# Two rows of the modulation's first quarter weighted by TensorE products instead of VectorE

## What is computed

```python
mod = jax.nn.silu(c) @ ada_w[layer] + ada_b[layer]          # (1, 1024) @ (1024, 6144)
shift1, scale1, gate1, shift2, scale2, gate2 = jnp.split(mod[:, None, :], 6, axis=-1)
h = rmsnorm(x, norm1_w[layer]) * (1 + scale1) + shift1
... = jnp.split(h @ w_in[layer], split_at, axis=-1)
```

## Time and profile before

| | |
|---|---|
| median of 3 runs | 894.42 us (894.19 to 894.9) |
| the profiled execution | 894.87 us |
| its span (first to last instruction) | 893.1 us |
| TensorE busy | 876.5 us, 98% |
| VectorE busy | 498.3 us, 56% |
| ScalarE busy | 365.6 us, 41% |
| DMA, mean over the span | 127 GB/s |

### The profile page before, as it was taken

One profiled execution on the slowest core, in us unless ns is written; L12 is line 12 of the kernel. 1 busy time (PEld: TensorE's weight loads), 2 busy tenths in 40 slices (PEclk: granted clock), 3 DMA queues, 4 the chain that ended last, 5 costly groups with the idle time before them and its releaser, 6 DMA issues.

```text
span 893.1 us, 13455 instructions
## 1 busy us (share of the span) xinstructions
PE 876.5 (98%) x5425; PEld 749.0 (84%) x5425; DVE 498.3 (56%) x599; ACT 365.6 (41%) x464; POOL 37.6 (4%) x40
## 2 busy tenths in 40 slices
PE   6999999999999999999999999999999999999997
PEld 5998878899898988888888898888888888888886
DVE  6778884646473748423445666555555556433337
ACT  6551226784534372522223344333333333322234
POOL 0010000000000000000122300000000000000004
PEclk9999999999999999999999999999999999999999
DMA  9975745115352454342424423333333332422202
GB/s 323 316 251 164 201 97 164 49 48 189 114 170 94 144 188 154 132 150 85 142 95 141 131 60 95 94 94 94 94 94 94 94 94 94 134 101 94 94 0 96
DMA packets 117141, 113.03 MB, mean 127 GB/s; under 512 B 7412, under 2 KB 107126, under 8 KB 114663
## 3 DMA queue, kind: packets, MB, share of 16 engines
q1 hardware_dynamic: 116375, 110.21, 39.6%
q10 hardware_dynamic: 720, 2.16, 0.7%
HBM read 104.80 MB, written 4.21 MB: 122 GB/s over the span
## 4 chain that ended last, share of the span: by engine, by line
PE 88%; DVE 4%; DMA 3%; SPq 2%; ACT 1%; issue 1%; DVEq 0%; ACTq 0%
PE bank L1835 25%; PE bank L1836 25%; PE bank L1837 25%; PE bank L2342 1%; PE bank L2176 1%; DMA ada_in<-in_ada_w_dram 1%; SPq L520 1%; PE bank L2016 1%; PE bank L2104 1%; PE bank L2181 1%; PE bank L2144 1%; DMA raw<-in_w_in_dram 1%; PE bank L1989 1%; PE bank L1870 1%; PE bank L2011 1%
## 5 line engine op out<-in xcount | busy, mean ns | idle before, releaser
L1835 PE MATMUL bank<-h_hi,w_hi 128*128 128x512 f32 x672 | 264.2, 393 | 0.9 <-DVE w_lo L1274 0.9
L1837 PE MATMUL bank<-h_hi,w_lo 128*128 128x512 f32 x672 | 261.6, 389 | 0.0
L1836 PE MATMUL bank<-h_lo,w_hi 128*128 128x512 f32 x672 | 261.6, 389 | 0.0
L1835 PEld LDWEIGHTS bank<-h_hi,w_hi 128*128 128x128 f32 x672 | 126.2, 188 | 27.5 <-DVE w_lo L1274 1.1
L1837 PEld LDWEIGHTS bank<-h_hi,w_lo 128*128 128x128 f32 x672 | 126.1, 188 | 26.5
L1836 PEld LDWEIGHTS bank<-h_lo,w_hi 128*128 128x128 f32 x672 | 126.2, 188 | 25.6 <-issue 0.2
L1267 DVE TENSOR_TENSOR w_lo<-raw,w_hi 128x2048 fp32r<-128x2048 f32 (+2 forms) x44 | 81.0, 1852 | 88.6 <-ACT w_hi L694 88.6
L1274 DVE TENSOR_TENSOR w_lo<-raw,w_hi 128x2048 fp32r<-128x2048 f32 x31 | 71.1, 2293 | 86.4 <-ACT w_hi L702 86.4
L1774 DVE SCALAR_TENSOR_TENSOR conv<-bank,vecs,conv 128x511 f32<-128x511 f32 x88 | 65.6, 748 | 66.2 <-ACT conv L1108 60.7
L702 ACT ACTIVATE w_hi<-raw 128x2048 fp32r<-128x2048 f32 x31 | 59.1, 1907 | 69.3 <-PE bank L1837 69.3
L694 ACT ACTIVATE w_hi<-raw 128x2048 fp32r<-128x2048 f32 (+2 forms) x42 | 67.9, 1631 | 44.4 <-DMA raw<-in_w_in_dram 34.7
(11 more groups left out here) (272 smaller groups left out, 1227.5 us busy)
## 6 DMA issues: line engine op xcount, KB each, us to landing
raw<-in_w_up_dram SPq DMA_DIRECT2D x44, 512.0 KB, 4.7
raw<-in_w_in_dram SPq DMA_DIRECT2D x17, 1024.0 KB, 5.3
raw<-in_ada_w_dram SPq DMA_DIRECT2D x16, 1024.0 KB, 5.5
raw<-in_w_in_dram SPq DMA_DIRECT2D x22, 512.0 KB, 5.6
raw<-in_w_down_dram SPq DMA_DIRECT2D x22, 512.0 KB, 4.2
ada_in<-in_ada_w_dram SPq DMA_DIRECT2D x16, 512.0 KB, 9.5
raw<-in_w_gla_branch_dram SPq DMA_DIRECT2D x4, 1024.0 KB, 5.1
raw<-in_w_out_dram SPq DMA_DIRECT2D x4, 1024.0 KB, 5.2
```

Source lines behind the costliest of these rows:

```text
L1835: pe.matmul(out_ap, wh, xh, start=first, stop=False, skip_group_check=True)
L1836: pe.matmul(out_ap, wh, xl, start=False, stop=False, skip_group_check=True)
L1837: return pe.matmul(out_ap, wl, xh, start=False, stop=last, skip_group_check=True)
```

## The change

For quarter 0, blocks 6 and 7 are taken off VectorE and put into `DIRECT[0]`. `FIRST_SUMS` now ends with block 5 in both halves, so VectorE does 6 instead of 8 steps per half. In `first_shift_scale` TensorE first takes, once silu(c) and the second half of the quarter are there, blocks 6 and 7 with their columns of `c_silu` (2 blocks x 2 column groups x 4 strips = 16 matmuls per half), then waits for VectorE's step of block 5, and sums block 0 with the ones as before. No transfer and no instruction of ScalarE, GpSimd or SP is changed.

```diff
-DIRECT = {1: range(5, KT), 2: range(6, KT), 3: range(0)}
-ADA_STEPS = [2 * KT] + [KT - len(DIRECT[j]) for j in range(1, KT // 2)]
-FIRST_SUMS = [(0, range(0, 4)), (1, range(0, 2)), (0, range(4, 8)), (1, range(2, 3)), (1, range(3, 8))]
+DIRECT = {0: range(6, KT), 1: range(5, KT), 2: range(6, KT), 3: range(0)}
+ADA_STEPS = [2 * (KT - len(DIRECT[0]))] + [KT - len(DIRECT[j]) for j in range(1, KT // 2)]
+FIRST_SUMS = [(0, range(0, 4)), (1, range(0, 2)), (0, range(4, 6)), (1, range(2, 3)), (1, range(3, 6))]
...
             def first_shift_scale(kk):
 
                 pe.wait_ge(ones_set, 1)
-                pe.wait_ge(ada_step, FIRST_AT[kk, KT - 1])
+                pe.wait_ge(silu_done, 1)
+                pe.wait_ge(ada_landed[1], 32)
                 if kk > 0:
                     pe.wait_ge(first_mod, 1)
-                for n in (kk, kk + 2):
-                    last = column_sum(bank[7], n, ada_rows(0, 0)[:, n * P:(n + 1) * P], ones[:, 0:1], n == 0, True)
+                for row in (*DIRECT[0], 0):
+                    if row == 0:
+                        pe.wait_ge(ada_step, FIRST_AT[kk, DIRECT[0][0] - 1])
+                    for n in (kk, kk + 2):
+                        last = column_sum(bank[7], n, ada_rows(0, row)[:, n * P:(n + 1) * P],
+                                          ones[:, 0:1] if row == 0 else c_silu[:, row:row + 1],
+                                          n == 0 and row == DIRECT[0][0], row == 0)
                 last.then_inc(first_ps if kk == 0 else mod1_ps, 1)
```

## The result

| | before | changed |
|---|---|---|
| median, same chip | 894.79 us (20 runs, 893.79 to 895.42) | 894.89 us (20 runs, 894.04 to 901.0) |
| profiled execution, span | 894.87, 893.1 | 894.97, 893.2 |

The ratio is 1.0026 (95% interval 1.0016 to 1.0037): the change makes the kernel slower by 0.26%, though its median hardly moves. The reason is in the single executions, and no number of this kernel can be understood without it: eleven of the 20 took 894.04 to 894.97 us (median 894.29, that is 0.5 less than before), nine took 899.5 to 901.0 (median 900.43), and nothing lay between. The mean of all 20 is 897.06 against 894.72 before, which is the 0.26%. Their mean granted clock differs too, 0.998 to 1.000 against 0.994 to 0.996. No execution of the kernel before, in five groups of 20 to 31, was above 895.8.

A forecast was written before the change was run, and what follows sets the result against it. The prediction took TensorE, busy 98% of the span, as the bound; -1.01 + 0.27 - 0.27 + 0.73 = -0.3 us took the median from 894.42 to 894.1 us, with an 8-in-10 range of 893.2 to 895.0.

The forecast's parts named there:

- Step 1, half 0: Quarter 0's first column sum: two VectorE rows fewer let TensorE start 1.01 us earlier; 32 added records cost 0.27 us.
- the 25 ns of the Trainium skill: Minimum start-to-start distance of matmuls; by it the 32 added records would cost 0.8 us per half, an estimate of 894.7.
- Step 2, half 1: Quarter 0's second column sum: no gain, 0.27 us added to TensorE, swallowed by 0.47 us of slack in the wide product.
- Step 3, who stops the shift: Start of quarter 1: weight landings fixed at 25.91 and 28.89 us cut the 1 us gain to 0.28 us.
- my wait: Quarter 1: new waits for landings, VectorE 0.6 to 0.9 us before L1191, TensorE about 0.5 us before L1870.
- my first rival: Quarter 1's landings don't hold; landing 0.8 us earlier, the whole 1.0 us comes through: 893.4 us; chance 0.13.
- Step 4: From quarter 1's sums to the end: everything behind moves by the same 0.3 us, and no DMA is added.
- anything else, the clock among it: Rival for any other cause, such as a fall from the granted 2.4 GHz; no size given; chance 0.02.
- The sum: Whole kernel: -1.01 (half 0) + 0.27 - 0.27 (half 1) + 0.73 (waits for fixed landings) = -0.3 us.

The follow-up runs named there:

- half 1 alone: The change made only in half 1, blocks 6 and 7 of half 0 staying on VectorE, against the kernel before; 895.86 us, ratio 1.0017.
- the products alone: The kernel before plus the 16 added products per half, sent to columns nobody reads, with all eight VectorE steps kept; 894.2 us, ratio 0.9995.
- before padded: The kernel before with 128 waits for a semaphore long set (64 instructions) at the start of TensorE's program; 895.9 us, ratio 1.0017.
- half 0: As a run: the change made only in half 0, half 1 as in the kernel before; 895.56 us, ratio 1.0012.
- the merged version without SP's wait: The change only in the first half, idle transposes at four places merged into wider products, SP's transfers not held back; 894.2 us, ratio 0.9995.
- the late kernel: The changed kernel with two of five idle transposes ahead of half 1's column sums replaced by one 512-column product; 894.24 us, ratio 0.9997.

## Why the prediction was wrong

The forecast was no difference; I gave 0.93 to "within 0.2%" and 0.04 to slower, and it is slower by 0.26%. The median, 894.89, lies in the range, but that is little comfort, since it stands between two groups that it describes badly.

**Step 1, half 0: the price was right, the occasion was not.** 32 added records cost 0.28 us (I had 0.27 from quarter 1's 8.4 ns), and the 25 ns of the Trainium skill that I weighed against it is not seen here. The wait of 1.11 us that they were to fill is a matter of the execution. It was 1.11 where TensorE started at 6.7 us, 0.39 in the second trace of before, where it started at 7.6, and in the traces of the changed kernel the start was 6.9 to 8.1. In the profiled execution of the changed kernel the tokens' transposes, not VectorE, come last at this place, and the 1.0 us of the step was worth nothing (16.70 for the transposes, 18.05 for the sum). With an early start (6.9, the execution of 893.16 us) the order came as forecast: the added products began at 16.93, the ones at 17.20. But VectorE's rows began earlier there too, at 15.32. In both traces of before the column sum came 2.20 us after that start (15.74 to 17.94, 15.95 to 18.15), so all eight steps would have let TensorE go at 17.52 there (an estimate), and the gain is 0.3 us, not 1.0. No trace of the changed kernel shows the full one. I took one trace's slack for the kernel's.

**Step 2, half 1: right.** From the start of half 1's sums to that of quarter 1's sums TensorE takes 29.39 - 22.14 = 7.25 us before, 29.51 - 22.25 = 7.26 with the change and 29.31 - 22.05 = 7.26 with half 1 alone, the added 0.27 us included. The slack behind it swallows them. The total of half 1 alone doesn't test the step: its trace has a stall of 1.65 us at an edge near 44 us, which is more than its 1.1 us of loss.

**Step 3, who stops the shift: not seen in any trace, and the landings aren't fixed.** In none of the five traces of the changed kernel does VectorE's first row of quarter 1 or TensorE's first product there wait for a landing. In the profiled execution VectorE began quarter 1 at 26.24 and the sums at 29.51, at about the old places, which was the late start and not my wait. In the execution of 893.16 us the landings, by issue plus time to landing, were 25.06 and 28.14 against my 25.91 and 28.89. VectorE began at 25.39 and the sums at 28.66, without a wait. The stream of weights isn't fixed from one execution to the next; the two landings moved by 0.85 and 0.75 us. This was my first rival (0.13), and its 893.4 is near that one execution, though the 1.0 us that it lets through wasn't there.

**Step 4 is the step that failed.** It said that nothing is added to DMA, and that everything behind moves by the same 0.3 us. TensorE's 128 more instructions are themselves brought by DMA, half a block of 256, and they moved the edges of the blocks against the work. The count was in sight ("32 records" for 16 calls, and the instruction queue is a line of the page), but I counted instructions only by the time that they run. The edge moved from 39.9 us, where its block had begun to come 8 us ahead, to 30.8 us, where the block comes 0 to 0.3 us late in short executions and 3.7 us late in the long one that was traced. Padding shows that the place of an edge alone can cost time: 64 instructions that do nothing made the kernel before slower by 0.17%, with a stall of 1.54 us at an edge predicted ahead. And with the edge moved out of the sums by the same padding the changed kernel had no long execution in 11. That the edge suffices for the long executions isn't shown: the products alone have it at the same place and had none.

**The clock.** I gave "anything else, the clock among it" 0.02, since the new wait was to be 0.5 us at most. The clock did fall, after a wait of 3.74 us that I hadn't foreseen, and made 2.3 of the traced long execution's 6.4 us.

**The sum.** Short executions: 894.29 against 894.79, so -0.5 us where I had -0.3. Long ones: +5.6. With nine in 20 long: 0.55 x (-0.5) + 0.45 x 5.64 = +2.26 us, which is 0.25%, and 0.26% was measured. That the short ones come near my -0.3 doesn't confirm my sum: the products alone, where nothing starts earlier, lie 0.6 us under their before as well.

**What stays open.** Only one long execution has a trace, so that the others have the same stall is concluded from their time and their granted clock (0.994 to 0.996 in all nine). Why the block's transfer starts at 27.5 to 28.7 us in one execution and at 32.24 in another isn't known: TensorE's time doesn't decide it, and holding the weights back didn't abolish it. The late start isn't peculiar to the long execution, though. In the six traces where this edge falls only at 34.8 us or later (both of before, before padded, half 0, half 1, and the merged version without SP's wait) the block's transfer began at 31.7 to 32.3 us as well, as the stream ran out; there nobody missed it. In these six TensorE passed the edge ahead of it, at 449, at 29.5 to 30.1 us, and in the changed kernel at 27.6 to 28.8 (28.61 in the long execution, 28.81 in a short one). Nor is it known why the products alone and the late kernel, with the same edge, had no long execution in 21, where the changed kernel had 15 in 31. The removed VectorE steps are what sets the products alone apart from the changed kernel, but the late kernel has them removed too and had no long execution in 10.

## What to carry to other kernels

Where an engine runs without a gap, count the instructions that a change adds ahead of a critical place, not only their time, and look in the trace for stalls by "issue" inside a group of like instructions: in these traces they marked the edges of the instruction blocks, and padding by idle instructions, put where they delay nothing, shows whether an edge is the cause. Take a wait's length from more than one execution when it hangs on a start that wanders by a microsecond. And look at the single times: a median that moved by 0.1 us and a profile of a short execution hid nine executions in 20 that were 6 us longer.

## What the runs showed of the hardware that was not expected

- TensorE's program comes in transfers of 16 KB, 256 instructions each. A transfer took 1.15 us beside full queues (28.27 us, the changed kernel) and 1.11 with the queues nearly empty (32.24 us, the long execution), and where TensorE stood waiting its instructions ran 2.4 to 2.7 us after its start. Stalls by "issue" stood after instructions 449, 705 and 961.
- Such a transfer shares the DMA engines with the data (share of the data 1.05 beside it). For the block behind instruction 705 it started at 27.5 to 28.7 us in the short executions of the changed kernel, the products alone and the late kernel, and only as the data's stream ran out, at 31.7 to 32.3 us, in the long execution and in six traces of kernels that reach this edge later.
- A stall of 3.74 us was followed by 6.8 us at half the clock; stalls of 1.38, 1.54 and 1.65 us were not followed by any such stretch.
- Waits for a semaphore long set aren't free at the head of TensorE's program: two of them took 0.106 us. 256 of them delayed the first matmul to 14.9 us; 128 left it at 8.0 to 8.1, where kernels without them began at 6.7 to 8.1.
